# Loading the context group's query weights ahead of its output projection, and running eight expert rows before the sample norm

## The chip, the cores and the metric

The kernel runs on one core of one Trainium2 chip. The metric is device time in microseconds (us) of one execution; lower is better. 0.2% of the time before is 8.8 us.

## What is computed

The program is one step of a two-layer network over two groups of tokens: 128 context tokens (one block of 128) and 512 sample tokens (four blocks). Both groups share all weights. In each layer a mixer (layer 0: convolution and attention; layer 1: Fourier and short convolution) is followed by a channel mixer that looks up experts by product keys:

```python
def peer(h, wq, keys, u_tab, v_tab):          # per block of 128 tokens
    q = (xb @ wq).reshape(n, PEER_HEADS, 2, PEER_HALF)
    s = jnp.einsum('nhpd,hpkd->nhpk', q, keys_f)
    sv, si = lax.top_k(s, PEER_TOPK)           # 16 of 128 keys, twice
    ...
    fv, fi = lax.top_k(cand, PEER_TOPK)        # 16 of the 256 pairs
    ue = jnp.take(u_tab, eidx, axis=0)         # 16 rows of 1024 per token and head
    act = jax.nn.gelu(jnp.einsum('nhkd,nd->nhk', ue, xb))
    ve = jnp.take(v_tab, eidx, axis=0)
    return jnp.einsum('nhk,nhkd->nd', gate * act, ve)
```

There are 2 layers, 5 blocks, 8 heads and 16 experts: 1280 "rows", each of which gathers 128 rows of `peer_u` and 128 rows of `peer_v` (1 MB together) for the 128 tokens of a block.

## The kernel before, in words

**Segments, steps and rows.** A segment is the expert lookup of one block in one layer (0 to 9; segment 0 is the context block of layer 0). It has 8 steps (one per head) of 16 rows. Five engine programs are written by hand in the same order of work; each calls its own `rows(n)` at the same places, so that `n` rows are woven between two pieces of the mixer's work. The numbers stand in `RATES`, by layer and group. The mixer of the sample group in layer 0 runs inside segment 0 and the start of segment 1.

**What a row is, per engine.** GpSimd gathers a u tile into `u_ring` (8 buffers) and a v tile into `v_ring` (8 buffers); its order is fixed in `step`: four u gathers, then four v gathers that lag by 8 rows. A u gather waits until VectorE has done the dot product that used its buffer (`dots_done`); the first v gather of a step waits for ScalarE's `spread_indices` (`idx_v_done`). VectorE does the dot (`dot`, line 1714), at row 15 of a step the top-k of the step two further on (`topk`), at row 6 `weigh`, and at rows 10, 13, 0 and 4 a `diagonal` (the weights that TensorE needs). ScalarE does at row 4 `late` (gelu, exp and a load of scores), at row 8 `spread_weights`, at row 12 `spread_indices`. TensorE, at every fourth row, adds four weighted v tiles to `ps_v` (line 931, 16 matmuls), 24 rows behind. `topk` ends with a write of `idx`, which waits until ScalarE has spread the indices of the step two before.

**Weights.** SyncE (SP) issues the weight loads in program order, each a slice of 256 columns (1 MB), into slots. `w_slots` has three slots; before the gathers begin, `v_ring` gives slots 3 to 6 and `seg_bufs` slots 7 and 8 (`slot_view`). Which slice goes where, and whose last reader it waits for, is set by `plan_weights`. In `prep` each slice of `peer_wq` comes with its 128 KB of `peer_keys`.

**Around the change.** In the context group of layer 0 the order is: mixer, `mix_out` (output projection, line 1168), `norm` for `h2T`, `scores` slices 0 and 1, top-k of steps 0 and 1, then segment 0 starts: `scores` slices 2 to 7 on TensorE and ScalarE beside `rows(16)` on VectorE. Then comes the sample group: `norm` for `hT` (4 blocks), `even_a` (four chunks `vg`, which need weight slices `win` 0 and 2, then 1 and 3; line 1015), `even_qkv` (four blocks; slices 4, 5, 6; line 1047), `attend` block 0 with the convolution's taps, `conv_norm`, `mix_out`, `norm` for `h2T`, `scores` (8 slices), and `attend` block 1. In that block, after head 4, `next_segment` runs what is left of segment 0.

## Time and profile before

| | us |
|---|---|
| median of 3 runs | 4412.31 (4406.25 to 4415.29) |
| the profiled execution, its own time | 4403.28 |
| its span, first to last instruction | 4401.5 |

The page of the profile gives over the whole span: VectorE busy 61%, GpSimd 55%, TensorE 50%, ScalarE 24%; 1579 MB moved at a mean of 359 GB/s; a mean granted TensorE clock of 0.69 of full speed. In stretches with no mixer the 16 DMA engines move 409 GB/s; in segment 0, where the sample group's mixer runs, they move 147 to 394 GB/s in stretches of 25 us.

How to read it: a timeline row gives the start, the length, the engine and line, output and inputs, and in brackets how long the engine had been idle and what ended that. A row of the SP queue is the issue of a transfer, not its landing. The number of a row of work (row 0 to 127 of segment 0) isn't in the trace; it follows from counting line 1714.

### The profile page before, as it was taken

To read this page: it belongs to the slowest core of one execution; us is meant where nothing else is said; L and a number is where in the kernel's file an instruction comes from. 1 tells how busy PE (TensorE), PEld (TensorE's weight loads), DVE (VectorE), ACT (ScalarE), POOL (GpSimd) and SP (SyncE) were. 2 spreads that over 40 slices of the span, in tenths; PEclk is the share of its full clock that TensorE was granted. 3 is DMA by queue.
4 is the path that set the end of the run, shared out by engine and by line. 5 is a ranking of instruction groups with operands and counts; after the bars stand their busy time and mean duration, and the time that the engine had idled before them with its cause. 6 is when DMAs were issued, how large, how long until landed. Compare 5 with 4: busy or idle time off the path is not lost.

```text
span 4401.5 us, 39752 instructions
## 1 busy us (share of the span) xinstructions
PE 2218.3 (50%) x11314; PEld 1066.7 (24%) x11314; DVE 2696.5 (61%) x6958; ACT 1068.6 (24%) x3554; POOL 2436.0 (55%) x2564
## 2 busy tenths in 40 slices
PE   6667566667834433334653397535853333333333
PEld 4545243334412100002430134303420000000000
DVE  3546947877455666675457545475566676767672
ACT  1132223232311222221222212221322222222221
POOL 0134545455554676775367443474467776777774
PEclk8879677678966655556775599757876565556656
DMA  9688898879999999999899988999999999999997
GB/s 292 201 292 299 289 319 303 307 274 385 362 381 386 397 408 409 409 409 361 321 401 409 351 298 302 339 409 343 376 374 409 409 408 403 402 403 400 409 402 299
DMA packets 576690, 1579.06 MB, mean 359 GB/s; under 512 B 49870, under 2 KB 237230, under 8 KB 576342
## 3 DMA queue, kind: packets, MB, share of 16 engines
q0 software_dynamic: 368640, 1342.34, 78.8%
q1 hardware_dynamic: 183744, 213.28, 14.3%
q10 hardware_dynamic: 24086, 20.92, 1.4%
q8 instruction: 88, 1.44, 0.1%
q14 instruction: 132, 1.08, 0.1%
HBM read 1550.16 MB, written 26.18 MB: 358 GB/s over the span
## 4 chain that ended last, share of the span: by engine, by line
DMA 30%; PE 18%; POOL 14%; issue 10%; DVE 8%; ACT 2%; SPq 1%; POOLq 0%; ACTq 0%; DVEq 0%
DMA v_ring<-in_peer_v_dram,idx_v 13%; POOL v_ring L870 8%; PE ps_box L1015 7%; DMA u_ring<-in_peer_u_dram,idx 6%; PE ps_v L931 6%; POOL u_ring L860 6%; DMA w_slots<-in_w_mod_dram 3%; DVE u_ring L1714 2%; DMA w_slots<-in_peer_keys_dram 2%; PE ps_box L1168 1%; DMA w_slots<-in_w_out_odd_dram 1%; DMA w_slots<-in_w_in_odd_dram 1%; PE ps_box L1150 1%; DMA xa<-XM 1%; PE ps_box L972 1%
## 5 line engine op out<-in xcount | busy, mean ns | idle before, releaser
L1714 DVE CUSTOM_DVE_ANT_0 u_ring<-u_ring,h_cur 128x1024 f32<-128x1024 f32 x1280 | 1532.9, 1216 | 628.9 <-DMA u_ring<-in_peer_u_dram,idx 612.0
L860 POOL DMA_INDIRECT u_ring<-in_peer_u_dram,idx x1280 | 1216.2, 950 | 1137.7 <-DVE act_v L1714 605.4
L931 PE MATMUL ps_v<-v_ring,w_diag 128*32 128x512 f32 x5120 | 1011.5, 930 | 1485.3 <-DMA v_ring<-in_peer_v_dram,idx_v 1346.7
L870 POOL DMA_INDIRECT v_ring<-in_peer_v_dram,idx_v x1280 | 1219.5, 953 | 809.0 <-PE ps_v L931 434.6
L931 PEld LDWEIGHTS ps_v<-v_ring,w_diag 128*32 128x32 f32 x5120 | 195.5, 146 | 2210.6 <-issue 1587.0
L1015 PE MATMUL ps_box<-HT,w_slots 128*128 128x128 f32 (+2 forms) x1728 | 473.9, 437 | 61.3 <-DMA w_slots<-in_w_in_odd_dram 32.5
L1312 ACT ACTIVATE w_v<-w_tok 32x4 f32<-32x4 f32 x1280 | 265.5, 207 | 806.0 <-DVE w_tok L1772 774.5
L1015 PEld LDWEIGHTS ps_box<-HT,w_slots 128*128 128x128 f32 x1728 | 293.2, 214 | 248.6 <-issue 152.1
L1322 ACT ACTIVATE idx_v<-idx 32x4 uint32<-32x4 uint32 x1280 | 265.5, 207 | 235.2 <-PE ps_v L931 220.2
L1328 ACT ACT_TABLE_LOAD x79 | 101.4, 1283 | 372.4 <-DVE act_v L1714 354.4
L1723 DVE TENSOR_TENSOR w_diag<-w_v,eye 128x128 f32<-128x128 f32 x320 | 92.0, 288 | 142.2 <-ACT w_v L1312 125.7
L1168 PE MATMUL ps_box<-w_slots,CAT 128*128 128x256 f32 x576 | 141.3, 407 | 51.6 <-DMA w_slots<-in_w_out_odd_dram 38.8
L1168 PEld LDWEIGHTS ps_box<-w_slots,CAT 128*128 128x128 f32 x576 | 116.4, 205 | 85.3 <-issue 45.4
L1959 DVE SCALAR_TENSOR_TENSOR HT<-AR,HT 128x128 f32<-128x128 f32 (+1 forms) x360 | 129.8, 432 | 0.0
L1334 ACT ACT_TABLE_LOAD x79 | 101.4, 1283 | 92.3 <-DVE neg_max L1746 91.1
L972 PE MATMUL ps_box<-w_slots,AR 128*2 128x128 f32 x768 | 65.4, 343 | 102.2 <-DMA w_slots<-in_w_mod_dram 94.3
L1714 DVE DVE_READ_ACCUMULATOR2_ANT act_v<- 128x1 f32 x1280 | 104.7, 82 | 0.0
L2045 DVE TENSOR_TENSOR AR<-ps_box,BC 128x256 f32<-128x256 f32 x40 | 16.9, 421 | 139.5 <-PE ps_box L1168 139.5
L1772 DVE SCALAR_TENSOR_TENSOR w_tok<-gelu_v,ex_rec,ex 128x16 f32<-128x16 f32 x80 | 18.8, 235 | 119.7 <-issue 114.4
L1095 PE MATMUL ps_box<-AR,HT 128*128 128x64 f32 x336 | 61.3, 344 | 57.0 <-ACT HT L1502 55.6
L1015 PE MATMUL ps_box<-CAT,w_slots 128*128 128x128 f32 x512 | 77.3, 317 | 15.3 <-ACT XM L1567 14.2
L1508 ACT ACTIVATE HT<-ps_box 128x640 f32<-128x640 f32 (+1 forms) x40 | 24.8, 619 | 243.9 <-PE ps_box L1088 243.9
(191 smaller groups left out, 2279.0 us busy)
## 6 DMA issues: line engine op xcount, KB each, us to landing
w_slots<-in_peer_wq_dram SPq DMA_DIRECT2D x48, 1024.0 KB, 13.2
w_slots<-in_w_mod_dram SPq DMA_DIRECT2D x34, 1024.0 KB, 15.5
u_ring<-in_peer_u_dram,idx POOLq DMA_INDIRECT x1280, 12.2
v_ring<-in_peer_v_dram,idx_v POOLq DMA_INDIRECT x1280, 12.1
w_slots<-in_w_in_odd_dram SPq DMA_DIRECT2D x16, 1024.0 KB, 16.9
w_slots<-in_w_out_odd_dram SPq DMA_DIRECT2D x12, 1024.0 KB, 24.8
v_ring<-in_w_mod_dram SPq DMA_DIRECT2D x11, 1024.0 KB, 12.1
s_buf<-sc ACTq DMA_DIRECT2D x78, 128.0 KB, 5.9
```

Source lines behind the costliest of these rows:

```text
L860: pool.indirect_dma_start(out=u_ring[:, k % NU, :], out_offset=None, in_=u_rows, in_offset=bass.IndirectOffsetOnAxis(ap=idx[:, h % 2, k:k ...
L870: pool.indirect_dma_start(out=v_ring[:, k % NV, :], out_offset=None, in_=v_rows, in_offset=bass.IndirectOffsetOnAxis(ap=idx_v[:, h % 2, k: ...
L931: last = nc.tensor.matmul(ps_v[QUARTER * q:QUARTER * q + QUARTER, 512 * half:512 * half + 512], w_diag[:, c % GROUPS, q, :], v_ring[:, (r ...
L972: last = nc.tensor.matmul(out[32 * j:32 * j + 2, :], ct[:, c, :], w[:, c, j * P:(j + 1) * P], start=(c == 0), stop=(c == DC - 1))
L1015: last = nc.tensor.matmul(out, w[:, c, col:col + P], h[:, c, :], start=(c == 0), stop=(c == DC - 1))
L1168: last = nc.tensor.matmul(box[:, 0:WC], cat(b)[:, c, :], w[:, c, :], start=(c == 0), stop=(c == 7))
L1312: last = nc.scalar.activation(dst, src, ACT.Copy)
L1322: last = nc.scalar.activation(dst, src, ACT.Copy)
L1328: nc.scalar.activation(gelu_v[:, h % 2, :], act_v[:, h % 2, :], ACT.Gelu_apprx_tanh).then_inc(gelu_done, 1)
L1334: nc.scalar.activation(ex[:, h % 4, :], fv[:, h % 2, :], ACT.Exp, bias=neg_max[:, h % 2:h % 2 + 1], accum_out=ex_sum[:, h % 4:h % 4 + 1]). ...
L1714: nc.vector.tensor_tensor_reduce(u_ring[:, k % NU, :], u_ring[:, k % NU, :], h_cur[:, :], 1.0, 0.0, ALU.mult, ALU.add, act_v[:, h % 2, k:k ...
L1959: ins = nc.vector.scalar_tensor_tensor(out[:, c, :], src, cw[:, c, j:j + 1], out[:, c, :], ALU.mult, ALU.add)
```

## The change

It has five parts.

1. In `plan_weights` the eight `peer_wq` slices of the context group in layer 0 get slots 0 to 6 and 0 again (`WQ_SLOTS`), so that slices 3 to 6 lie in `v_ring`, and the order of slots after them starts anew. Their keys come as one transfer of 1 MB into `seg_bufs[:, 2:4]`.
2. On SP, the keys and slices 0 to 3 are issued before the loads of the next norm's rows (`bc_ffn`), slices 4 to 6 before `out_end` (the store of `xa`, which waits for the output projection), slice 7 behind the store of `hs`. `load_seg(0)`, whose buffers now hold the keys, moves behind the last slice that reads them.
3. GpSimd waits, between step 0 and step 1, until TensorE has used slice 6, the last one in `v_ring`.
4. ScalarE runs its 16 rows of step 0 (of which only `spread_indices` does anything) between `scores` slices 3 and 4, not behind slice 7.
5. `EARLY_ROWS`: all engines run 8 more rows before the sample group's norm; `RATES` gives them back: 4 rows for each chunk of `even_a` where it was 5, 2 in `conv_norm` where it was 4, and the last 2 rows in `next_segment` are gone.

```diff
+WQ_SLOTS = (0, 1, 2, 3, 4, 5, 6, 0)
-RATES = {(0, SMP): {"norm": 1, "vg": 5, "vg_end": 2, "qkv": 5, "attend": (3, 3, 3, 3), "conv_norm": (4, 4), "out": (1, 2),
+RATES = {(0, SMP): {"norm": 1, "vg": 4, "vg_end": 2, "qkv": 5, "attend": (3, 3, 3, 3), "conv_norm": (2, 4), "out": (1, 2),
+EARLY_ROWS = 8
...
-    early = len(FIRST_ORDER) + 4
+    first = len(FIRST_ORDER) + 4
...
-        slot = n % NWA if n < early else (n - early) % NW
+        if n < first:
+            slot = n % NWA
+        elif n < first + 8:
+            slot = WQ_SLOTS[n - first]
+        else:
+            slot = (n - first - 8) % NW
...
+            def wq_first(first, end):
+                for s in range(first, end):
+                    load_weight(sp, ("wq", 0, CTX, 0, s), T["peer_wq"][0], s * WC)
...
             sp.wait_ge(S("mod_row", 0), 8)
+            sp.dma_start(seg_bufs[:, 2:4, :].rearrange("p n d -> p (n d)").rearrange("p (j d) -> p j d", d=P),
+                         T["peer_keys"][0].rearrange("h j k d -> k (h j) d")).then_inc(S("keys_in"), 16)
             rows_out(0, 1, 3, 6)
             rows_out(0, 0, 0, 2)
+            wq_first(0, 4)
...
             load_bc(0, CTX, 3, 1, "bc_ffn")
+            wq_first(4, 7)
             out_end(0, CTX, 0)
-            prep(0, CTX, 0)
+            sp.wait_ge(S("h2_tok", 0, CTX), 1)
+            sp.dma_start(hs[0], h2_tile(0, CTX, 0)).then_inc(S("hs_out", 0, CTX), 16)
+            wq_first(7, 8)
+            sp.wait_ge(S("hs_out", 0, CTX), 16)
+            sp.wait_ge(S("xa_out", 0, CTX), 16)
+            load_h(0)
 
             mix_in(0, SMP)
             prep_end(0, CTX, 0)
+            box, use = boxes[("kyT", 0, CTX, 0, 7)]
+            sp.wait_ge(box_ready[box], use + 1)
+            load_seg(0, 0, CTX)
             even_in(SMP)
...
+            box, use = boxes[("q", 0, CTX, 0, 13)]
+            pool.wait_ge(box_ready[box], use + 1)
...
             start(0)
             third(0, 0, CTX)
+            rows(TOPK)
             scores(0, CTX, 0, 4, 8)
-            rows(TOPK)
+            rows(EARLY_ROWS)
             all_stored(0, CTX, 0)
             norm(0, SMP, "hT")
```

TensorE and VectorE have `rows(TOPK + EARLY_ROWS)` where they had `rows(TOPK)` at the start of segment 0.

How instructions stand on two engines shows it. On the SP queue, around the end of the context group's mixer (`modrow` is the table of modulation rows, `BC` its broadcasts, `in_peer_wq` and `in_peer_keys` the query weights and keys), before:

```order
L639 DMA modrow<-u_ring 2x12x128 [waits mod_row_0,mod_taken_0]
L639 DMA modrow<-u_ring 2x12x128
L639 DMA modrow<-u_ring 2x8x128 x2
L651 DMA BC<-modrow 128x1024 [waits mod_out_0,kv_out]
L651 DMA BC<-modrow 128x1024
L714 DMA xa<-XM 128x1024 [waits x_mixed_0_0]
L459 DMA w_slots<-in_peer_wq_dram 128x8x256 [waits wmod_read_0]
L461 DMA w_slots<-in_peer_keys_dram 128x2x128
```

and with the change:

```order
L800 DMA seg_bufs<-in_peer_keys_dram 128x16x128 [waits mod_row_0,mod_taken_0]
L649 DMA modrow<-u_ring 2x12x128 x2
L649 DMA modrow<-u_ring 2x8x128 x2
L469 DMA w_slots<-in_peer_wq_dram 128x8x256 [waits wmod_read_0] x3
L469 DMA v_ring<-in_peer_wq_dram 128x8x256 [waits wmod_read_0]
L661 DMA BC<-modrow 128x1024 [waits mod_out_0,kv_out]
L661 DMA BC<-modrow 128x1024
L469 DMA v_ring<-in_peer_wq_dram 128x8x256 [waits box_ready1]
L469 DMA v_ring<-in_peer_wq_dram 128x8x256 [waits box_ready0]
L469 DMA v_ring<-in_peer_wq_dram 128x8x256 [waits box_ready1]
L728 DMA xa<-XM 128x1024 [waits x_mixed_0_0]
L812 DMA hs<-CAT 128x1024 [waits h2_tok_0_0]
```

The keys and four slices stand ahead of the two `BC` loads, three more ahead of the store of `xa`, and only the eighth behind the store of `hs`.

On ScalarE, from the store of scores of slice 3 on (`AR` holds queries, keys and staged scores, `sc` is their place in memory), before:

```order
L1587 DMA sc<-AR 128x256 [waits box_free1]
L1567 ACTIVATE AR<-ps_box 128x256 [waits box_ready0,stage_out_0_0_0_1]
L1571 ACTIVATE AR<-ps_box 128x128 [waits box_ready1]
L1571 ACTIVATE AR<-ps_box 128x128 [waits box_ready0]
L1580 ACTIVATE AR<-ps_box 128x128 [waits stage_out_0_0_0_0,box_ready1]
```

and with the change:

```order
L1615 DMA sc<-AR 128x256 [waits box_free1]
L1350 ACTIVATE idx_v<-idx 32x4 [waits topk_done,stage_out_0_0_0_1]
L1350 ACTIVATE idx_v<-idx 32x4 x15
L1595 ACTIVATE AR<-ps_box 128x256 [waits box_ready0]
L1599 ACTIVATE AR<-ps_box 128x128 [waits box_ready1]
```

The spread of step 0's indices stands ahead of slice 4, no longer behind slice 7.

On ScalarE again, from the store of slice 7 to the first block of the sample norm (`CAT<-XM` is its square, `HT<-ps_box` the copy of a transposed block, `w_v` the spread weights), before:

```order
L1587 DMA sc<-AR 128x256 [waits box_free1]
L1322 ACTIVATE idx_v<-idx 32x4 [waits topk_done]
L1322 ACTIVATE idx_v<-idx 32x4 x15
L1435 ACTIVATE CAT,st<-XM 128x1024 [waits xm_in_0_1,stage_out_0_0_0_1,stage_out_0_0_0_0]
L1436 ACT_TABLE_LOAD
L1436 ACTIVATE st<-st,eps 128x1 [waits act_chain]
L1435 ACTIVATE CAT,st<-XM 128x1024
L1436 ACTIVATE st<-st,eps 128x1 [waits act_chain]
L1458 ACTIVATE HT<-ps_box 128x8x128 [waits box_ready0]
```

and with the change:

```order
L1615 DMA sc<-AR 128x256 [waits box_free1]
L1356 ACT_TABLE_LOAD
L1356 ACTIVATE gelu_v<-act_v 128x16 [waits dots_done]
L1362 ACT_TABLE_LOAD
L1362 ACTIVATE ex,ex_sum<-fv,neg_max 128x16 [waits negmax_done]
L1380 DMA s_buf<-sc 128x256 [waits topk_done]
L1463 ACTIVATE CAT,st<-XM 128x1024 [waits xm_in_0_1,stage_out_0_0_0_1,stage_out_0_0_0_0]
L1464 ACT_TABLE_LOAD
L1464 ACTIVATE st<-st,eps 128x1 [waits act_chain]
L1463 ACTIVATE CAT,st<-XM 128x1024
L1464 ACTIVATE st<-st,eps 128x1 [waits act_chain]
L1486 ACTIVATE HT<-ps_box 128x8x128 [waits box_ready0]
```

Gelu, exp and a load of scores now stand between the last slice and the norm, and `spread_weights` inside the norm; both stood in `even_a`.

## Rows read from the trace of the kernel before

**Rows 1.** The page's DMA queues: packets, MB, share of 16 engines.
```profile
q0 software_dynamic: 368640, 1342.34, 78.8%
q1 hardware_dynamic: 183744, 213.28, 14.3%
```

**Rows 2.** Windows: busy us per engine, granted PE clock, DMA share, GB/s.
```profile
150.00:175.00 25.00, 18.92 (x75) 15.69 (x74) 5.53 (x11) 5.21 (x8) 0.00 (x0) 0.75 0.00 1
...
250.00:275.00 25.00, 11.41 (x71) 9.86 (x70) 9.77 (x14) 13.16 (x37) 3.80 (x2) 0.70 0.76 260
...
350.00:375.00 25.00, 16.47 (x76) 9.53 (x74) 14.22 (x31) 7.49 (x23) 16.58 (x18) 0.93 0.95 351
```

**Rows 3.** Timeline of ScalarE: start us, us, operation, [idle before <-releaser].
```profile
234.14 0.38 ACT L1567 ACTIVATE AR<-ps_box 128x256 f32<-128x256 f32 x1 [6.39 <-DMA sc<-AR]
...
258.82 3.49 ACT L1322 ACTIVATE idx_v<-idx 32x4 uint32<-32x4 uint32 x16 [0.42 <-ACT AR L1580]
```

**Rows 4.** Timeline of VectorE, 262 to 269 us, same columns.
```profile
262.42 0.17 DVE L1764 TENSOR_SCALAR idx<-abf 128x16 uint32<-128x16 f32 x1 [19.94 <-ACT idx_v L1322]
...
265.19 0.16 DVE L1876 RECIPROCAL st<-st 128x1 f32<-128x1 f32 x1 [2.60 <-ACT st L1436]
...
267.85 1.21 DVE L1714 CUSTOM_DVE_ANT_0 u_ring<-u_ring,h_cur 128x1024 f32<-128x1024 f32 x1
```

**Rows 5.** Timeline of GpSimd, its gathers, 233 to 287 us.
```profile
233.46 0.94 POOL L860 DMA_INDIRECT u_ring<-in_peer_u_dram,idx  x1 [0.59 <-DVE act_v L1714]
...
269.34 1.94 POOL L860 DMA_INDIRECT u_ring<-in_peer_u_dram,idx  x1 [34.95 <-DVE act_v L1714]
...
285.69 0.94 POOL L870 DMA_INDIRECT v_ring<-in_peer_v_dram,idx_v  x1 [0.30 <-issue]
```

**Rows 6.** Timeline of the SP queue, loads of the sample projection's slices.
```profile
260.20 2.75 SPq L459 DMA_DIRECT2D w_slots<-in_w_in_even_dram  x3
...
314.29 40.73 SPq L459 DMA_DIRECT2D w_slots<-in_w_in_even_dram  x3
```

**Rows 7.** Timeline of TensorE, 282 to 376 us.
```profile
282.45 29.13 PE L1015 MATMUL ps_box<-HT,w_slots 128*128 128x512 f32 x64 [1.11 <-ACT HT L1458]
...
315.48 3.16 PE L931 MATMUL ps_v<-v_ring,w_diag 128*32 128x512 f32 x16 [3.89 <-DVE w_diag L1723]
322.24 15.97 PE L1015 MATMUL ps_box<-HT,w_slots 128*128 128x512 f32 x32 [3.59 <-issue]
338.14 1.92 PE L931 MATMUL ps_v<-v_ring,w_diag 128*32 128x512 f32 x16
...
375.78 14.08 PE L1047 MATMUL ps_box<-w_slots,HT 128*128 128x256 f32 x64 [2.66 <-DMA w_slots<-in_w_in_even_dram]
```

**Rows 8.** Timeline of VectorE in the sample attention, 432 to 473 us.
```profile
432.56 0.22 DVE L1919 RECIPROCAL st<-st 128x10 f32<-128x10 f32 x1 [2.90 <-ACT st L1486]
...
462.70 0.29 DVE L1728 MAX8 sv<-s_buf 128x8 f32<-128x128 f32 x1
...
472.16 0.17 DVE L1764 TENSOR_SCALAR idx<-abf 128x16 uint32<-128x16 f32 x1
```

**Rows 9.** Timeline of TensorE where the sample output projection starts.
```profile
566.86 9.71 PE L1168 MATMUL ps_box<-w_slots,CAT 128*128 128x256 f32 x32 [6.79 <-ACT CAT L1528]
```

**Rows 10.** Timeline of ScalarE, SP queue, TensorE, 586 to 626 us.
```profile
586.48 1.06 ACT L1435 ACTIVATE CAT<-XM 128x1024 f32<-128x1024 f32 x1 [16.29 <-DVE XM L2048]
...
595.56 0.71 SPq L725 DMA_DIRECT2D hs<-CAT  x1
...
606.71 0.38 ACT L1567 ACTIVATE XM<-ps_box 128x256 f32<-128x256 f32 x1 [11.54 <-DMA hs<-CAT]
...
625.98 0.69 PE L1182 MATMUL ps_box<-ident,w_slots 128*128 128x128 f32 x2 [10.75 <-DMA w_slots<-in_peer_keys_dram]
```

**Rows 11.** Timeline of VectorE and TensorE, 679 to 697 us.
```profile
679.00 0.82 DVE L1970 TENSOR_REDUCE st<-ps_box 128x1 f32<-128x640 f32 x1 [18.47 <-PE ps_box L1077]
...
696.14 1.30 PE L1088 MATMUL ps_box<-ident,HT 128*128 128x128 f32 x5 [8.16 <-DVE HT L1990]
```

More of the change, by code:

```diff
@@ L188, in mix @@
             for s in range(8):
-                order.append((("wq", l, g, q, s), ("q", l, g, q, 2 * s + 1), 2))
+                order.append((("wq", l, g, q, s), ("q", l, g, q, 2 * s + 1), 1 if (l, g) == (0, CTX) else 2))
     mix(0, CTX)
@@ L448, in weight_keys @@
         def weight_keys(key):
+            if key[1:3] == (0, CTX):
+                at = 2 * P * key[4]
+                return seg_bufs[:, 2:4, :].rearrange("p n d -> p (n d)")[:, at:at + 2 * P].rearrange("p (j d) -> p j d", j=2)
             return w_slots[:, weights[key][0], DC * WC:DC * WC + 2 * P].rearrange("p (j d) -> p j d", j=2)
@@ L727, in prep @@
                         sp.wait_ge(S("xa_out", l, g), 16 * hi)
-                        if (l, g) == (0, CTX):
-                            load_h(0)
-                            load_seg(0, 0, CTX)
-                        elif g == SMP:
+                        if g == SMP:
                             load_h(5 * l + 1 + q)
@@ L884, in step @@
                             gather_v(i - 1, h - 1, k - V_LAG)
-            for i in range(16):
-                step(i // 8, i % 8, first=i == 0)
+            step(0, 0, first=True)
+            box, use = boxes[("q", 0, CTX, 0, 13)]
+            pool.wait_ge(box_ready[box], use + 1)
+            for i in range(1, 16):
+                step(i // 8, i % 8)
             with Segments(pool, 2, 4, per_seg) as seg:
@@ L1178, in scores @@
                     w = weight(pe, ("wq", l, g, q, s))
+                    if (l, g) == (0, CTX):
+                        pe.wait_ge(S("keys_in"), 16)
                     kr = weight_keys(("wq", l, g, q, s))
@@ L1217, in _ @@
             scores(0, CTX, 0, 2, 8)
-            rows(TOPK)
+            rows(TOPK + EARLY_ROWS)
             turn_h(0, SMP, "hT", "h_tok")
@@ L1621, in _ @@
             third(0, 0, CTX)
+            rows(TOPK)
             scores(0, CTX, 0, 4, 8)
-            rows(TOPK)
+            rows(EARLY_ROWS)
             all_stored(0, CTX, 0)
@@ L2070, in _ @@
             start(0)
-            rows(TOPK)
+            rows(TOPK + EARLY_ROWS)
             norm(0, SMP, "hT")
```

## The prediction

> **What bounds the kernel now.** I read the page first, then windows of 25 us over the first 800 us, then each engine's timeline from 120 to 745 us, since all that the change touches lies there. From the start of segment 1 on, both programs are the same, every wait there is on another engine or on a transfer, and nothing waits for a fixed time: what segment 0 gains or loses should reach the end whole. So the sum is made of the points where segment 0 waits.
>
> Two idle stretches stand out. Between 150 and 175 us the transfers are idle (share 0.00) while the context group's mixer ends [rows 2]. Later VectorE waits 19.94 us with the top-k of step 2 finished but for its write of `idx`, because ScalarE spreads step 0's indices only behind slice 7, at 258.82 [rows 3, 4]. GpSimd in that time stands still for 34.95 us, since no dot frees a buffer [rows 5]. The reader is to see that it isn't the transfers that limit here: in 250 to 275 us they run at 260 GB/s [rows 2]. Behind it, in the sample mixer, limits alternate: TensorE in `even_a` (29.13 us of matmuls for two chunks, 15.97 for the third) [rows 7], then the landing of slices, then VectorE through `even_qkv` and `attend`, where a top-k takes 472.16 - 462.70 = 9.5 us [rows 8].
>
> **The change part by part.** All shifts are changed kernel minus before.
>
> *Early weights.* Some 9 MB of slices and keys move into the idle stretch. That alone gives little: slices 0 and 1 weren't waited for, and the first dots hang on two top-ks that hang on the projection. Slices 4 to 7 take ScalarE (258.8 - 234.1) / 4 = 6.2 us each with waits for keys in them [rows 3]; without these I take 5. ScalarE reaches slice 4 at 234.14, after 6.39 us for a store of scores [rows 3]; with fewer weights in the queues this store may come 0 to 3.5 us sooner. Add the 3.49 us spread and four slices: the last slice ends at about 254.5 to 258.5, against 258.8 before.
>
> *The new wait on GpSimd.* The gathers of step 1 (16 to 31) are held until slice 6 is used, about 6 us before the last slice ends: 248.6 to 252. Before, gathers up to 23 were out at 234.4 [rows 5]; this is what comes late in place of the spread. Behind it on GpSimd stands every later gather, v too. At 0.94 + 0.30 = 1.24 us a gather [rows 5] gather 23 is issued at 257.6 to 261 and lands an estimated 5 us later (a store through busy queues took 6.39), so dot 23 ends at 263.7 to 267. Of the 20 us that VectorE waited, the wait keeps most, but eight dots now lie in it.
>
> *The norm.* Before, VectorE starts it at 265.19 [rows 4]. ScalarE must now do gelu and exp first (about 4 us, two table loads), which ends at 258.5 to 263, and the norm's square and root take 2.9 (262.3 to 265.19) [rows 3, 4]: no later than the dots. Its four blocks are unchanged. In it TensorE now has the first v sum, 3.2 us at half clock [rows 7], and ScalarE a 3.5 us spread. `even_a` needs slices `win` 0 and 2, issued at about 260 as before [rows 6], but now beside some 20 gathers. I take a start 2.5 us later than 282.45 [rows 7]; bounds -1 (the store is quick) and +10.
>
> *even_a.* TensorE's chunks stay. Two v sums (rows 31 and 35 where one stood) lie about the first pair; the first adds 1.9 [rows 7], the second lies under the load of slice 3, which is issued when chunk 1 is done: that sets the start of chunk 2 at 322.24, 10.6 us behind 311.6 [rows 7]. The wait of 3.89 us on the diagonal goes, and is worth nothing, since the load ends last. The end of chunk 3 is then +1.9. Next come slices 5 and 6, issued by 314.29 + 40.73 = 355.0 [rows 6] and awaited until 375.78 [rows 7]: 21 us, with 18 gathers issued in 350 to 375 us at a transfer share of 0.95 [rows 2, 7], because a top-k (row 31) had dammed up the dots of chunk 2. It now falls into chunk 0, where VectorE is idle; I count 12 gathers in that stretch and take 3 us less. Together -1; bounds -6 and +2.
>
> *even_qkv.* With four rows more done, both rows 47 and 63, each with a top-k, fall in it, where one did. VectorE is the chain here: +9.5. The 2.90 us wait on ScalarE's root [rows 8] goes, as gelu and spreads move to blocks with cover: +6.6; bounds +3 and +9.5.
>
> *attend, block 0.* One top-k where two stood: -9.5, and with VectorE less full 1 us of other waits shows: -8.5; bounds -9.5 and 0.
>
> *conv_norm.* Two dots less (2.3 us), and row 88, a spread of 3.5 us on ScalarE just ahead of the last activation, moves forward into `attend`; a v sum moves behind the variance. The output projection waited 6.79 us for ScalarE here [rows 9]. -4.5; bounds -6 and 0.
>
> *mix_out and the second norm.* The v sum inside the four chunks moves behind them: -2. But row 95 with its top-k now stands between the mixed x (586.48) and the norm, 7.6 us more for the norm. ScalarE's slices don't start from the norm, however, but from the landing of the store of `hs`: it is issued at 595.56, 9.1 us after the mixed x, behind two slices, and lands 11 us later, at 606.71 [rows 10]. Issued 13.3 us after, with those slices mostly landed, it should take 5 to 10 us: -1 for this. -3 in all; bounds -6 and +7.6.
>
> *scores.* Eight slices with two rows each as before, limited by landings (10.75 us for one [rows 10]): 0; bounds -4 and +4.
>
> *attend, block 1, head 0.* The top-k of row 111 stood here, and TensorE waited 8.16 us for VectorE; now it falls into the slices, where VectorE is idle for 18.47 us at their end [rows 11]. -8; bounds -9.5 and 0.
>
> *next_segment.* Two dots fewer before segment 1, 1.14 us each at VectorE's pace: -2.3.
>
> Sum: 2.5 - 1 + 6.6 - 8.5 - 4.5 - 3 + 0 - 8 - 2.3 = -18.2 us. The profiled execution took 4403.28, 9 us under the median; its span would be 4383, its own time 4385, and the median 4412.3 - 18.2 = **4394 us**. As 0.2% (8.8 us) is about what a measurement of this kernel tells from no change, this is faster. A check from the other side: eight dots (9.2 us) and one top-k leave the stretches where VectorE is the chain, 18.7 us.
>
> **A rule against it.** In the load of slices 5 and 6 before, about 2 MB took 21 us beside gathers that never paused, near 100 GB/s [rows 6, 7]. The page's queues have mean packets of 3.6 KB for gathers and 1.2 KB for SP's loads [rows 1]. The Trainium skill ("DMA: Bandwidth & Descriptors", Queues, rings and completion order) says that each DMA engine goes round its queues by packet; one to one this would leave SP a quarter of 400 GB/s, and by that rule the trace agrees. With the gathers' burst on `win` 0 and 2 this rule alone would put the sum near -13.
>
> **The rivals.**
>
> *A. The burst holds up the first slices of the sample projection* (a chance of 0.2). Gathers 16 to 31 with v 0 to 7 now run without a pause from 250 to 280, where the trace has GpSimd idle. The segment's own loads (1 MB) and `win` 0 and 2 share with them. At the 21 us for 2 MB above, and 5 us for the segment's loads, `win` 2 lands at 286 to 290, so `even_a` starts 4 to 8 us late, and slice 3 may lose 2 more. Against it: the burst ends at about 280. Sum: -18.2 + 5 = about 4399, bounds 4395 to 4406.
>
> *B. The top-ks land on the path and none leaves it* (0.12, slower). The shift by four and two rows moves top-ks as follows: one into `even_qkv` (+6.6), one between mixed x and norm (+7.6 if the store of `hs` follows the norm by its 11 us as before). If block 0 of `attend` and head 0 of block 1 turn out to be held by TensorE and ScalarE and give nothing: 2.5 - 1 + 6.6 + 0 - 4.5 - 2 + 7.6 + 0 + 0 - 2.3 = +6.9, and with `conv_norm` giving nothing +11.4: 4419 to 4424. It decides when the two attentions give back less than 5 of their 16.5 us. Against it: VectorE has hardly a gap in them.
>
> *C. Little change* (0.18). Some of the gains are real but a landing ends last behind them: the slices of `scores` are limited by transfers, and if the same bytes need the same time whenever they start, the shift is halved or lost there: 4404 to 4416.
>
> *D. More* (0.1). Quick stores, the early slices also freeing the queues, bounds taken on the good side: -26 to -35, 4377 to 4386.
>
> The forecast itself has 0.4, with a range of 4386 to 4400.
>
> **How the numbers follow.** Faster by over 0.2% (under 4403.5): the forecast, D and nearly all of A give 0.4 + 0.1 + 0.18 = 0.68. Within 0.2%: C and the rest of A, 0.2. Slower: B, 0.12. The range leaves out the slower half of C and B at the top, and little below: 4379 to 4413.
>
> **What would show it.** In the changed kernel's profile: the loads of `peer_wq` between 141 and 171 us and a share above 0.7 in place of 0.00; ScalarE's first spread at 231 to 238; VectorE's write of the third `idx` without a wait at 239 to 243, then a wait of 9 to 14 us for the gather of row 16, ended by a transfer; GpSimd idle until about 250 and then 24 gathers in a row; `even_a` at 284 to 287; two top-ks in `even_qkv` and one in the first `attend`; no wait of TensorE on VectorE in the first head of block 1. The prediction is wrong if the wait for `win` 2 or for `hs` is longer than it was by more than 8 us, or if segment 0 ends at the same time as before with these steps as described, which would mean that a landing I took as hidden sets its end.

## The result, and the profile after

The changed kernel takes 4422.47 us (median of 8 runs, 4411.85 to 4426.40), the kernel before 4411.15 us (8 runs beside it, 4403.61 to 4415.41): ratio 1.0027, 95% interval 1.0017 to 1.0037, or some 11 us **slower**. I had forecast 18 us faster. The profiled execution took 4420.41 us with a span of 4418.6 us, at the same mean granted clock (0.69).

The early part went as forecast. Windows of the kernel after (columns as in [rows 2]):

```profile
150.00:175.00 25.00, 19.71 (x79) 16.50 (x77) 4.88 (x9) 5.49 (x9) 0.00 (x0) 0.73 0.89 291
250.00:275.00 25.00, 7.18 (x43) 6.03 (x42) 17.50 (x28) 13.55 (x35) 19.01 (x20) 0.61 1.01 390
275.00:295.00 20.00, 7.09 (x33) 4.11 (x34) 7.88 (x13) 5.99 (x10) 11.22 (x11) 0.59 1.04 395
350.00:375.00 25.00, 21.29 (x57) 8.25 (x55) 6.05 (x13) 5.96 (x10) 7.51 (x8) 0.93 0.57 200
```

The idle stretch of the transfers is filled (share 0.89 where it was 0.00), but from 250 to 295 us they are full: 390 GB/s, where [rows 2] had 260. Timelines of the kernel after, of ScalarE, VectorE, GpSimd and the SP queue, which answer to [rows 3 to 6]:

```profile
230.02 3.49 ACT L1350 ACTIVATE idx_v<-idx 32x4 uint32<-32x4 uint32 x16 [2.57 <-DMA sc<-AR]
...
252.34 1.22 DVE L1743 CUSTOM_DVE_ANT_0 u_ring<-u_ring,h_cur 128x1024 f32<-128x1024 f32 x1 [11.91 <-DMA u_ring<-in_peer_u_dram,idx]
...
275.49 0.16 DVE L1905 RECIPROCAL st<-st 128x1 f32<-128x1 f32 x1 [3.06 <-ACT st L1464]
...
247.72 0.94 POOL L883 DMA_INDIRECT u_ring<-in_peer_u_dram,idx  x1 [24.63 <-PE ps_box L1041]
...
260.44 17.74 SPq L469 DMA_DIRECT2D w_slots<-in_w_in_even_dram  x3
```

The spread is at 230.02, VectorE's wait is now for the gather of row 16, and GpSimd starts at 247.72 and then issues 28 gathers without a pause, until 284.6. That was in the forecast but for the length of the run of gathers: I had named 24, with an end at about 280. Then it goes another way. Timeline of TensorE after, which answers to [rows 7]:

```profile
294.66 16.53 PE L1041 MATMUL ps_box<-HT,w_slots 128*128 128x512 f32 x32 [7.60 <-DMA w_slots<-in_w_in_even_dram]
315.08 3.64 PE L957 MATMUL ps_v<-v_ring,w_diag 128*32 128x512 f32 x16 [3.89 <-DVE w_diag L1752]
318.65 14.80 PE L1041 MATMUL ps_box<-HT,w_slots 128*128 128x512 f32 x32
336.20 2.56 PE L957 MATMUL ps_v<-v_ring,w_diag 128*32 128x512 f32 x16 [2.75 <-DVE w_diag L1752]
338.89 14.90 PE L1041 MATMUL ps_box<-HT,w_slots 128*128 128x512 f32 x32
356.54 2.42 PE L957 MATMUL ps_v<-v_ring,w_diag 128*32 128x512 f32 x16 [2.75 <-DVE w_diag L1752]
358.89 15.15 PE L1041 MATMUL ps_box<-HT,w_slots 128*128 128x512 f32 x32
379.08 3.21 PE L957 MATMUL ps_v<-v_ring,w_diag 128*32 128x512 f32 x16 [5.04 <-DVE w_diag L1752]
...
601.64 6.35 PE L1194 MATMUL ps_box<-w_slots,CAT 128*128 128x256 f32 x16 [6.70 <-DMA w_slots<-in_w_out_even_dram]
```

`even_a` starts 12.2 us later than in [rows 7], behind a slice (`win` 2) that was issued right after 260.44 and lands some 34 us later. In it stand four v sums, and each waits for a diagonal (3.89, 2.75, 2.75 and 5.04: 14.4 us, against 6.1 before). And the last chunk of the output projection waits 6.70 us for slice `wout` 3, where there was no wait. VectorE's timeline in `even_qkv` shows where each block of tokens begins:

```profile
394.79 0.82 DVE L1944 TENSOR_TENSOR CAT<-CAT 128x640 f32<-128x640 f32 x1 [11.87 <-ACT AR L1511]
...
420.32 0.83 DVE L1944 TENSOR_TENSOR CAT<-CAT 128x640 f32<-128x640 f32 x1 [3.30 <-ACT AR L1511]
...
439.89 0.83 DVE L1944 TENSOR_TENSOR CAT<-CAT 128x640 f32<-128x640 f32 x1 [6.49 <-ACT AR L1511]
...
456.96 0.83 DVE L1944 TENSOR_TENSOR CAT<-CAT 128x640 f32<-128x640 f32 x1 [2.64 <-ACT AR L1511]
...
484.58 0.82 DVE L1999 TENSOR_REDUCE st<-ps_box 128x1 f32<-128x640 f32 x1 [5.09 <-PE ps_box L1103]
```

Blocks 0 and 3 hold a top-k (25.5 and 27.6 us) and block 2 none (17.1), but block 1, which has none either, takes 19.6 us and ends in 6.49 us of idle time.

With such starts (of the norm, `even_a`, the first block of `even_qkv`, the first head of `attend`, `mix_out`, ...) segment 0 can be cut into stretches. Each number is what a stretch adds to the shift against the kernel before, in us, and the last row is the sum, up to the copy of `h_cur` for segment 1 (730.08 before, 748.49 after). The other columns are kernels of the next section.

| stretch | after | e1 | e4 | e9 | e13 | e14 | e15 |
|---|---|---|---|---|---|---|---|
| up to the norm's start | -0.4 | -5.8 | +2.5 | -3.6 | -3.2 | -1.5 | -2.2 |
| norm, wait for `win` | +12.7 | 0 | +5.4 | +12.9 | +11.9 | +13.7 | +3.2 |
| `even_a`, first keys | +2.1 | +1.2 | -1.6 | -5.6 | -6.4 | +15.5 | -2.6 |
| `even_qkv` | +11.7 | 0 | +10.9 | +9.1 | +17.5 | +9.0 | +10.6 |
| `attend`, block 0 | -4.9 | +0.5 | -6.1 | -8.3 | -3.7 | -9.2 | -8.4 |
| `conv_norm` | -3.6 | -0.3 | -3.6 | -4.5 | -3.6 | -1.2 | -3.6 |
| `mix_out` | +5.0 | -0.2 | +4.8 | -0.4 | -0.2 | -4.1 | 0 |
| second norm, `scores` | -1.9 | -0.3 | -3.9 | -5.9 | +4.2 | +1.9 | -4.6 |
| `attend`, block 1, four heads | -2.1 | +2.2 | -3.3 | -1.2 | -3.7 | -1.2 | -2.4 |
| end of segment 0 | +18.4 | -2.8 | +5.1 | -7.4 | +12.7 | +22.8 | -10.1 |

A profile is one execution: e4 and a twin of it (e10) with the same program up to `conv_norm` start the norm 3.6 us apart, so a single entry is good to some 4 us. The last row has about the order of the medians and not their size: it is up to 10 us above the difference of the medians (after, e13 and e15 by 7 to 10), as the profiled execution of the kernel before was 8 us faster than its median, and that of e13 the slowest of its 12.

### The profile page after: what moved, and what is told of

It reads as the page before. It is cut to its first block, busy times and chain, and to the rows that moved or that the text cites. A ratio compares the mean times of both kernels' runs of the same rounds, so it can differ in the third digit from the quotient of the medians.

```text
span 4418.6 us, 39748 instructions
## 1 busy us (share of the span) xinstructions
PE 2234.1 (51%) x11314; PEld 1071.4 (24%) x11314; DVE 2698.2 (61%) x6958; ACT 1068.6 (24%) x3554; POOL 2444.9 (55%) x2564
## 4 chain that ended last, share of the span: by engine, by line
DMA 30%; PE 18%; POOL 11%; DVE 10%; issue 9%; ACT 2%; SPq 1%; POOLq 0%; DVEq 0%; ACTq 0%
DMA v_ring<-in_peer_v_dram,idx_v 13%; DMA u_ring<-in_peer_u_dram,idx 7%; POOL v_ring L893 7%; PE ps_box L1041 7%; PE ps_v L957 6%; POOL u_ring L883 5%; DMA w_slots<-in_w_mod_dram 3%; DVE u_ring L1743 3%; DMA w_slots<-in_peer_keys_dram 2%; PE ps_box L1194 1%; DMA w_slots<-in_w_out_odd_dram 1%; DMA w_slots<-in_w_in_odd_dram 1%; SPq L471 1%; PE ps_box L1176 1%; PE ps_box L998 1%
## 5 line engine op out<-in xcount | busy, mean ns | idle before, releaser
L1041 PE MATMUL ps_box<-HT,w_slots 128*128 128x128 f32 (+2 forms) x1600 | 453.6, 446 | 48.5 <-DMA w_slots<-in_w_in_odd_dram 26.2
L1041 PEld LDWEIGHTS ps_box<-HT,w_slots 128*128 128x128 f32 x1600 | 273.1, 211 | 236.7 <-issue 156.5
L2074 DVE TENSOR_TENSOR AR<-ps_box,BC 128x256 f32<-128x256 f32 x40 | 16.9, 423 | 145.5 <-PE ps_box L1194 145.5
L1041 PEld LDWEIGHTS ps_box<-CAT,w_slots 128*128 128x128 f32 x512 | 78.2, 243 | 21.0 <-ACT XM L1595 11.7
## 6 DMA issues: line engine op xcount, KB each, us to landing
u_ring<-in_peer_u_dram,idx POOLq DMA_INDIRECT x1280, 12.1
v_ring<-in_peer_v_dram,idx_v POOLq DMA_INDIRECT x1280, 12.1
v_ring<-in_w_mod_dram SPq DMA_DIRECT2D x11, 1024.0 KB, 12.1
```

The source lines that it names most:

```text
L1041: last = nc.tensor.matmul(out, w[:, c, col:col + P], h[:, c, :], start=(c == 0), stop=(c == DC - 1))
```

## Experiments

Fifteen kernels, each timed beside the kernel before.

**Loads or rows.** Two theories at first: that gathers in a burst keep `win` 2 from landing, or that the rows stand badly. e1 takes the rows out of the changed kernel, e2 adds to the kernel before the earlier spread alone, e3 adds spread, eight rows and rates without the loads, e4 issues `win` 2 and 1 early.

```diff
 # e1, from the changed kernel
-                   "vg": 4, ... "conv_norm": (2, 4)
+                   "vg": 5, ... "conv_norm": (4, 4)
-EARLY_ROWS = 8
+EARLY_ROWS = 0
 # e2, from the kernel before (e3: also rows(EARLY_ROWS), and the new rates)
+            rows(TOPK)
             scores(0, CTX, 0, 4, 8)
-            rows(TOPK)
 # e4, from the changed kernel; even_in leaves out 2 and 1
             mix_in(0, SMP)
+            for s in (2, 1):
+                load_weight(sp, ("win", 0, SMP, s), T["w_in_even"][0], s * WC)
```

> The changed kernel without its eight early rows: EARLY_ROWS is 0 and the rates of vg and conv_norm are those of before, so that only the earlier weights and keys, GpSimd's wait and the earlier spread are left. Two theories of the 11.3 us that the change lost. Burst theory: the run of gathers from 250 us on keeps the slices win 0 and 2, issued at 260 us, from landing, and even_a's late start (12.2 us) is nearly the whole loss. Then even_a starts here not before 284 us although VectorE has eight dots less to do ahead of the norm and ends the norm by 276, and the kernel takes 4410 to 4418. Rows theory: the loss comes from where the v sums and top-ks of the eight rows fall (w_diag waits in even_a, two top-ks in even_qkv, a late wout 3). Then even_a starts at 276 to 282, later stretches are as in the kernel before, and the kernel takes 4402 to 4408.

> The kernel before, with ScalarE's spread of step 0's indices moved ahead of slices 4 to 7 and nothing else. Gathers 16 and on then go out as dots free their buffers, from about 242 us, in place of 269. Both theories: the norm can start when ScalarE has done slice 7, at 258 to 262 in place of 265.2. Burst theory: win 0 and 2, issued at 260, are met by fewer gathers (16, mostly issued by 262), so that even_a starts at 276 to 281 and the kernel takes 4404 to 4409, faster by 2 to 7 us. Rows theory says nothing else here. If the landing of win 2 sets even_a's start at 282 or later all the same, neither the burst nor the norm's start is what counts, but the time of issue at 260.

> The kernel before, with the earlier spread, the eight early rows and the new rates, but with weights and keys where they were and with no wait on GpSimd. Gathers 16 to 23 are out by 234, so that the early dots can run at 243 to 253, in VectorE's idle time. Burst theory: even_a starts at 280 to 285 and the rest is as I first worked it out, so that the kernel takes 4393 to 4403, the best so far. Rows theory: even_a starts at that time too, but the v sums wait for the diagonals of their own chunk (14 us in four waits in the changed kernel), even_qkv holds two top-ks and wout 3 comes late, so that the start of the x_mixed of mix_out is 6 to 12 us later against even_a's start than in the kernel before, and the kernel takes 4408 to 4420.

> The changed kernel, with the loads of win 2 and win 1 of the sample group issued behind the loads of the sample blocks, as soon as slices wq 1 and 2 are used (by about 220 us, 40 us ahead of before and ahead of the gathers). Their slots are free then. Only win 0 still waits for wq 7. Burst theory: with one slice in place of three beside the burst, even_a starts by 284 to 288, held by the norm's end (283.3) or by win 0, and 7 to 10 us come through to the end: 4412 to 4416. Rows theory: even_a starts as early, but the chunks then wait longer for diagonals and VectorE, and less than 4 us reach the end: 4418 to 4423.

Measured: e1 4408.23 us (ratio 0.9999, 0.9989 to 1.0009); e2 4406.70 (0.9994, 0.9985 to 1.0002); e3 4414.15 (1.0010, 1.0001 to 1.0020); e4 4415.43 (1.0012, 1.0004 to 1.0021). The loads, GpSimd's wait and the spread alone cost nothing and bring nothing that can be measured (e1, e2; VectorE starts e2's norm at 264.87, where 258 to 262 was expected, as the spread waits 6.22 us for a store of scores). Eight rows with the old loads are already slower than before (e3, where I had once forecast a gain), and early `win` slices give the changed kernel some 6 us back (e4, by the ratios). So both theories hold in part: by e4 the late slices are about half of the loss, and the rows are the other half.

In e1 the norm starts 5.8 us earlier than before, and TensorE then waits for no slice (`even_a` at 276.62). The late `win` of the changed kernel is thus not due to GpSimd's wait alone: without early dots only 8 gathers go out in a row, with them 28.

**Which of the rows.** e5 takes the rows out of the norm and puts five in each chunk of `even_a`; e6 has seven early rows in place of eight; e7 lightens `even_qkv`; e8 has no early rows and six in each chunk. All four have e4's early `win` slices.

```diff
 # e5                                    # e7 adds "qkv": 4, "conv_norm": (4, 4)
-{"norm": 1, "vg": 4,
+{"norm": 0, "vg": 5,
 # e6
-EARLY_ROWS = 8
+EARLY_ROWS = 7
 # e8, from e1
-{"norm": 1, "vg": 5,
+{"norm": 0, "vg": 6,
```

> e4_win_early (the changed kernel with win 2 and 1 loaded early) with no row in the sample norm and five in each chunk of even_a (norm 0, vg 5), so that after even_a the rows stand as in e4. Norm theory (from the traces of e1, e3 and e4): with eight early rows the norm starts about 8 us later than without, and in it the row that is a multiple of 16 plus 8 puts a spread of w_v (3.5 us) into ScalarE's way, so that the norm takes 21.1 us in place of 15.7. Without rows it takes 11 to 13 us: even_a starts at 280 to 283 in place of 290.4, the v sums no longer stand behind the last dot of their own chunk, and waits on w_diag fall from 14.4 to under 6 us: even_a ends 10 to 16 us earlier than in e4 and the kernel takes 4400 to 4408. Diagonal theory (the v sums' waits are what counts, the norm is hidden behind the landing of win 0): even_a starts at 286 to 290 and 5 to 8 us are won inside even_a: 4407 to 4412. If neither helps, VectorE's load alone sets the time and it takes 4413 to 4417.

> e4_win_early with seven early rows in place of eight (EARLY_ROWS 7): every v sum of even_a then stands behind the first row of a chunk, whose diagonal was made in the chunk before, and the weighing of row 24 (which waits for ScalarE's gelu behind slice 7) moves out of the stretch ahead of the norm. Diagonal theory: the four waits of v sums on w_diag (3.89, 2.75, 2.75, 5.04 us) go, even_a is 8 to 14 us shorter, and the kernel takes 4403 to 4408. Norm theory: only the start of the norm moves, by one dot and the wait on gelu, even_a's chunks stay 19 to 21 us apart, because VectorE's work on each chunk and not the v sum sets their distance: 4411 to 4415.

> e5_bare_norm with qkv 4 in place of 5 and conv_norm (4, 4) in place of (2, 4), so that even_qkv has rows 46 to 61 with one top-k, and from attend of block 0 on the rows stand as in the kernel before. If the chance placing of top-ks behind even_a costs nothing in sum (they only move), this gives what e5 gives less four dots in even_qkv, plus what block 0 of attend had gained: within 3 us of e5. If the late top-k between mixed x and norm (7.6 us) and the late wout 3 (6.3 us wait) are what the changed kernel loses behind even_a, this is 4 to 8 us faster than e5: 4394 to 4402.

> The other way round: early weights, early spread and early win 2 and 1, but no early rows at all (EARLY_ROWS 0, rates norm 0, vg 6, conv_norm (4, 4)), so that rows 16 to 39 lie in even_a and all behind it is as in the kernel before. Norm theory: the norm starts at 261 as in e1 and takes 11 to 13 us, so that even_a starts at 272 to 275, against 282.5 before and 276.6 in e1; six dots a chunk (6.9 us) still fit beside 14 us of matmuls, and the kernel takes 4398 to 4405, the fastest yet. Against it: if the landing of win 0, issued at 257, sets the start, even_a starts at 276 or later and nothing is gained over e1 (4408); if six dots and VectorE's own work on a chunk are more than 15 us, the chunks grow by 1 to 3 us each and it takes 4406 to 4412.

Measured: e5 4408.74 us (1.0002, 0.9989 to 1.0015); e6 **4397.43** (0.9973, 0.9961 to 0.9985); e7 4412.29 (1.0010, 0.9996 to 1.0023); e8 4424.39 (1.0035, 1.0019 to 1.0051). e5 takes the time of the diagonal theory, but not for its reason: `even_a` starts at 283.3, as the norm theory had it, 7.1 us ahead of e4, and the median follows (7 us under e4's). The further gain that the norm theory had inside `even_a` didn't come, as three v sums still wait for diagonals there (12.1 us together). e7, with the rows behind `even_qkv` as in the kernel before, is no faster than e5, so that by this run their new place costs nothing in sum: e7's profile is 15 us shorter than e5's in `even_qkv` and 5 in `mix_out`, and 13 us longer in `attend` of block 0 with `conv_norm`, 4 in the second norm and `scores`, and 5 in block 1. e8 is 12 us above even the slower of its two cases (4412): its v sums wait 7.66, 3.89 and 3.18 us, as six dots stand ahead of or beside each diagonal. The surprise is e6: one row fewer is worth 17 us, more than all four waits on diagonals.

**One row alone.** e9 is the changed kernel with seven early rows and nothing else, e11 the same on the old loads (e3). e10 takes two rows out of `conv_norm` of e4. e12 puts the v sums right with three early rows.

```diff
 # e9 and e11
-EARLY_ROWS = 8
+EARLY_ROWS = 7
 # e10, from e4
-"conv_norm": (2, 4)
+"conv_norm": (0, 4)
 # e12, from e1
-EARLY_ROWS = 0            "vg": 5, "vg_end": 2
+EARLY_ROWS = 3            "vg": 4, "vg_end": 3
```

> The changed kernel with EARLY_ROWS 7 in place of 8 and nothing else. In e6 this one row gave 17 us over e4 (4397.4 against 4415.4). Theory now: a v sum on TensorE that stands in the same step as the dot that makes its diagonal on VectorE stalls TensorE; with eight rows all four of even_a's do, with seven none but the last; and one row fewer brings row 91's v sum into mix_out's first chunk and row 95's top-k behind the second norm. Then this kernel has even_a's chunks without waits on w_diag, no wait for wout 3, and takes 4398 to 4408; the late landing of win 2 stays, so that it is 3 to 8 us behind e6 (4397). If early win 2 and 1 were what made seven rows work, it takes 4412 or more.

> e4_win_early (eight early rows) with conv_norm (0, 4) in place of (2, 4): two rows fewer ahead of mix_out, so that from there on the rows stand as in the kernel before (v sum of row 91 inside mix_out, row 95's top-k behind the second norm, row 111's in the first head of attend, two rows left for next_segment). If the late wout 3 (6.25 us wait) and that top-k (7.6 us ahead of the norm) are part of the loss, mixed x comes 5 to 8 us earlier than in e4 and the kernel takes 4406 to 4412; the top-k of row 111 takes back up to 8 us of it in block 1. If what is behind even_qkv costs nothing in sum, it takes 4413 to 4418 as e4.

> e3_rows_only (the kernel before with the earlier spread and the new rates, old loads, no wait on GpSimd) with seven early rows in place of eight. Theory now: the four waits on w_diag and the late wout 3 go as in e6, and the kernel takes 4397 to 4404, so that the early loads of weights and keys are worth nothing for the gain (e6: 4397). If the early loads count (norm and even_a earlier), it takes 4405 to 4410.

> e1_no_early_rows with three early rows (EARLY_ROWS 3) and rates vg 4, vg_end 3: the v sums of rows 27, 31, 35 and 39 stand behind the first row of a chunk, as in e6, and all behind even_a is as in the kernel before. Only three dots lie ahead of the norm, in time in which VectorE waits anyway (gathers 16 to 18 land by 254, ScalarE's square root for the norm comes at 259.4 in e1). So the norm starts at 260 to 262 and even_a at 276 to 278 as in e1, even_a is 3 to 6 us shorter than in e1, and the kernel takes 4398 to 4405. If it takes 4406 or more, the v sums' place is worth little by itself and the gain of e6 came from behind even_qkv.

Measured: e9 4401.29 us (0.9981, 0.9970 to 0.9992); e10 4418.52 (1.0022, 1.0013 to 1.0030); e11 4402.24 (0.9976, 0.9966 to 0.9986); e12 4416.62 (1.0014, 1.0004 to 1.0023). So the row is what counts, and the early loads are not needed for it (e11 is as fast as e9). TensorE's waits of 286 to 400 us, kernel after (engine, line, waited for: us in total, times, longest):

```profile
PE ps_v L957 <- DVE w_diag L1752: 14.4, 4, 5.0
PE ps_box L1041 <- DMA w_slots<-in_w_in_even_dram: 7.6, 1, 7.6
```

and the same stretch of e9:

```profile
PE ps_box L1041 <- DMA w_slots<-in_w_in_even_dram: 10.9, 1, 10.9
PE ps_box L1041 <- issue: 5.3, 1, 5.3
PE ps_v L957 <- DVE w_diag L1752: 4.3, 1, 4.3
```

The late slice is there in both; the waits on diagonals are gone but for one. e10 shows the other half: with row 91 in `mix_out` the wait for `wout` 3 is gone there too (`mix_out` 5.3 us shorter than e4's), but more than that is lost again. Row 111's top-k falls into block 1 again (3.4 us in the profiles), and the second norm and `scores` take 6.9 us more, with a wait of 8.76 us for the keys of the third slice that e4 doesn't have. My expectation had only the first of these. e12 is a miss, and it speaks against the v sums as the whole story: of their waits in `even_a` one of 2.04 us is left, and the kernel is still some 7 us slower than e1 by the ratios. Its profile has gelu and exp inside the norm, where TensorE waits 5.98 us, so that `even_a` starts at 285.38, and slices 5 and 6 are waited for 6.95 us, in e1 1.02 us. 3.9 us of the later start were there at ScalarE's first spread already (231.44 against 227.54), with the same program up to it, so they are the difference of two executions.

**V sums or dots.** In e13 TensorE alone is one row behind (23 rows at the start, 24 on VectorE and ScalarE), in e14 one ahead (24 against 23). e15 is e9 with `win` 2 and 1 issued once `wq` 4 is used.

```diff
 # e13, TensorE's program only
-            rows(TOPK + EARLY_ROWS)
+            rows(TOPK + EARLY_ROWS - 1)
 # e14, EARLY_ROWS = 7, TensorE's program only
+            rows(TOPK + EARLY_ROWS + 1)
 # e15, from e9; even_in leaves out 2 and 1
             mix_in(0, SMP)
+            box, use = boxes[("q", 0, CTX, 0, 9)]
+            sp.wait_ge(box_ready[box], use + 1)
+            for s in (2, 1):
+                load_weight(sp, ("win", 0, SMP, s), T["w_in_even"][0], s * WC)
```

> The changed kernel with TensorE alone one row behind: it goes through 23 rows at the start where VectorE and ScalarE go through 24, so that dots, weighings and top-ks stand where they do in the changed kernel and only the v sums stand one row later against them (each of even_a's stands a chunk after its diagonal). Alignment theory: of the 21 us between eight and seven early rows (4422 and 4401), the part that is due to v sums is even_a's (8.5 us by the traces), up to 3 us in even_qkv, and wout 3 with the v sum ahead of mix_out (5.4 us): 4405 to 4412. Top-k theory: what seven rows gain lies in where the top-ks and dots stand (rows 63, 95 and 111), and this takes 4415 to 4422.

> The reverse: seven early rows on VectorE and ScalarE, as in e9_seven_rows_alone, but eight on TensorE, so that each v sum of even_a again stands in the chunk in which its diagonal is made, while dots and top-ks stand as in e9. Alignment theory: the waits on w_diag come back, with one more dot to wait for, and wout 3 is late again: 12 to 18 us of e9's gain are lost, 4413 to 4422. Top-k theory: 4401 to 4406 as e9.

> e9_seven_rows_alone with win 2 and win 1 issued when slice wq 4 is used, at about 237 us: in e9 the transfers move 57 GB/s between 235 and 250 us, while the gathers are held back, and TensorE waits 10.87 us for win 2, until 291.80. In e4 the same two loads at 195 us slowed the stores of scores on which ScalarE waits (5.9 in place of 2.7 us) and put the norm's start 3 to 6 us back. Issued here 2 MB land by 246. Burst theory: even_a starts at 282 to 286 in place of 291.8 and the kernel takes 4392 to 4398. If a later landing or VectorE then sets the pace, and the 8 us are taken back in even_qkv and attend, it takes 4399 to 4402.

Measured: e13 4413.83 us (1.0007, 0.9996 to 1.0017); e14 4428.63 (1.0039, 1.0025 to 1.0053); e15 **4390.62** (0.9960, 0.9946 to 0.9975), 20 us faster than before in its own comparison and the fastest of all. e13 lies between its two theories, e14 6 us above the upper bound of the alignment theory, and e15 just under its range. TensorE's waits in e14, same stretch:

```profile
PE ps_v L957 <- DVE w_diag L1752: 28.5, 4, 13.4
PE ps_box L1041 <- DMA w_slots<-in_w_in_even_dram: 8.1, 1, 8.1
```

With dots and top-ks where e9 has them, putting the v sums one row forward costs 25 us. With the dots of the changed kernel, putting them one row back gives 9 us (ratio 1.0027 to 1.0007). Of the 20 us between eight rows and seven, a little under half is the v sums' own; the rest is where the dots and top-ks stand, and how the two meet: e13's profile has 6 us more than the changed kernel's in `even_qkv`, where a spread on ScalarE now waits for a late v sum. ScalarE and VectorE of e13:

```profile
438.45 3.49 ACT L1350 ACTIVATE idx_v<-idx 32x4 uint32<-32x4 uint32 x16 [9.32 <-PE ps_v L957]
...
442.30 0.22 DVE L1948 RECIPROCAL st<-st 128x10 f32<-128x10 f32 x1 [5.79 <-ACT st L1514]
```

In e15 `even_a` starts at 283.38 without a wait for a slice, 8.4 us earlier than in e9, and the median is 9 us better by the ratios (0.9981 to 0.9960, on 6 runs and with intervals that just overlap; the trace is the stronger evidence).

## Why the prediction was wrong

The terms of the forecast add up to -18.2 us and the stretches of the profile to +18.4, so the prediction is off by 36.6 us. Five steps make nearly all of it: the start of `even_a` (9.7), `attend` of block 1 (8.1), the output projection (7.0), `even_qkv` (5.1) and `attend` of block 0 (3.6). The step that failed most is the first: the overlap of slice `win` 2 with the gathers, for which the sum had a start 2.5 us later and the runs show 12.2. Behind part of the rest stands a wait that the sum put at nothing, that of the v sums for their diagonals.

**Right:** that the idle stretch fills, that the last slice ends a few microseconds sooner (253.8, just under my 254.5), VectorE's 12 us for the gather of row 16, GpSimd's wait, the norm's unchanged start, two top-ks in `even_qkv`, 4.5 us in `conv_norm` (3.6), the 7.6 us that row 95's top-k puts ahead of the second norm and the quicker store of `hs` that takes them back (-1.0 in sum, as forecast), no change in `scores`, the 2.3 us of `next_segment` (head 4 up to the copy of `h_cur` takes 4.7 us where it took 7.0), and that what segment 0 has at its end comes through (18.4 us there, 17.1 in the span).

**"A start 2.5 us later"** measured 12.2, over the upper bound of 10. The sum followed the norm and gave the burst a chance of 0.2 and 4 to 8 us as rival A. The rate was right: 2 MB of slices and 1 MB of the segment's own in 34 us are 88 GB/s, near the 100 that I had read off slices 5 and 6. My burst was too short: I had it end at about 280, and 3 MB at 100 GB/s from 260.4 would have been 291. The count of 24 gathers left out four u gathers for which the norm's dots free the buffers. Rival A's mechanism is shown by e15 (`win` 2 issued in a pause, no wait) and is worth 8 to 9 us, in e15 against e9. DMA queues of the kernel after, 270 to 294.66 us (packets, MB, share of 16 engines; q0 has the gathers, q1 SP's loads):

```profile
q0 software_dynamic: 2088, 7.61, 79.2%
q1 hardware_dynamic: 2088, 2.11, 24.5%
```

Packet for packet the two queues got the same number, and with 3.6 KB against 1.0 KB a packet SP's share of the bytes is 22%. The Trainium skill ("DMA: Bandwidth & Descriptors", Queues, rings and completion order) has the queues take turns by packet, and this trace agrees. My own sign of being wrong, a wait for `win` 2 over 8 us longer than before, wasn't even reached: the wait is 7.60 us, as TensorE came out of the norm 4.6 us later than before. Also left out of the sum was the norm itself: a spread for row 24 stands on ScalarE between its roots, and VectorE waits 3.06 us there, but the landing hides it.

**"The wait of 3.89 us on the diagonal goes"**, and is worth nothing, is the mechanism that failed. It did not go, there were four such waits (14.4 us in place of 6.1). A diagonal of row 29 is made by VectorE in the very chunk behind which TensorE's v sum of row 31 stands, so that TensorE must sit out VectorE's first dots of the chunk. With eight rows and four a chunk, every v sum of `even_a` stands behind the last row of its chunk; with seven, behind the first, and its diagonal is a chunk old. I counted how many v sums stand there and what each costs in matmuls (1.9 us), and not which row of the step makes what they need. `even_a` to the first keys measured +2.1 (I had -1), against -5.6 in e9. e13 and e14 show it: moving the v sums alone moves this stretch by 8.5 and 21 us.

**"even_qkv +6.6"** measured 11.7. The second top-k costs its 9.5 (e9: +9.1), and the 2.9 us that I took off for a root wait did not come: another wait, 3.9 us longer than it was, took its place (6.49 at the end of block 1, where 2.64 stood). A wait that moves isn't a wait that goes.

**"attend, block 0, -8.5"** measured -4.9 and in e9 -8.3, so the price was right for rows that stand well. **"mix_out -2"** measured +5.0: slice 3 is issued at 588.07, into gathers with no pause above 2.5 us, and lands 13.6 us later, where before it was issued at 573.15 in a pause of GpSimd of 7.7 us and nobody waited. In e9 and e13, with the v sum of row 91 inside `mix_out`, the wait is gone. That a pause of the gathers is what makes the slice quick fits all 17 kernels: the four with a wait (after, e3, e4, e5) have no pause above 4.0 us near the issue, the others one of 6.6 us or more (e14 too, with its v sum ahead: 597.32, in a pause of 9.4 us). It was not tried by itself.

**"attend, block 1, head 0, -8"** gave 4.5 us in head 0 (16.9 us to 12.4), and heads 1 to 3 took them back (27.2 to 31.8). Timeline of ScalarE after, in heads 2 and 3:

```profile
724.23 3.48 ACT L1340 ACTIVATE w_v<-w_tok 32x4 f32<-32x4 f32 x16
...
734.45 3.48 ACT L1350 ACTIVATE idx_v<-idx 32x4 uint32<-32x4 uint32 x16
```

Each spread stands a head earlier than before (713.76 in head 3, 724.98 in head 4). Head 2, which had none, takes 10.2 us in place of 7.2, head 1 10.4 in place of 9.0, and head 3 11.2 in place of 11.0; in all three VectorE now waits for TensorE, by up to 2.08 us at once where it was at most 1.02. So ScalarE's spread fits as the cause of most of it, but that was not tried; I had taken one wait of 8.16 us for the whole story.

Rival B (top-ks land on the path, none leaves it) had the right range, 4419 to 4424, by luck and not by its cause: top-ks did leave both attentions. The two causes that were found, the burst and the v sums, are A and one that I hadn't listed. What stays open is the part of the row's 20 us that e13 does not give back, 11 us by the ratios. Between e9 and e13 the table has it in `even_qkv` (8.4 us), `attend` of block 0 (4.6) and the second norm and `scores` (10.1), which with e13's slow profiled execution is more than the medians have; between e9 and the changed kernel the same three are 2.6, 3.4 and 4.0. Which dot or top-k is to blame in each was not separated.

## What to carry to other kernels

Where two engines interleave the same list of background work by count, a shift by one item can change which engine waits for which. So look, for each item that has a partner on another engine, whether the partner's half stands in an earlier step, and try the neighbours of the number chosen (8 lost 11 us, 7 won 9) before judging the idea. That alone isn't enough: with three early rows (e12) the v sums stood well too, and nothing was won. And a load that is short of time goes out in a pause of the gathers: the same two slices cost nothing at 237 us and 8 us at 260, but with them at 195 us ScalarE waited 5.8 to 5.9 us for its second store of scores in all six such kernels, and 2.1 to 3.2 us in the kernels with early `wq` slices that issue them later.

## What the runs showed of the hardware

TensorE often pays for a wait twice. Its v sum of 16 matmuls takes 1.92 us behind a chunk of matmuls, and behind the four waits of 2.75 to 5.04 us in the changed kernel 2.42 to 3.64 us, so that such a wait cost up to 1.7 us more than its length. It isn't so each time: behind a wait of 2.75 us in e4 and one of 3.18 us in e13 the v sum took 1.92 us. A chunk that follows a stretch in which TensorE mostly waits is slow as well: the first chunk takes 16.53 us in the changed kernel, behind the wait of 7.60 us, and 16.82 us in e15 directly behind the norm, with a wait of only 1.11 us, where e4's, with a v sum ahead of it, takes 14.00. The granted clock is 0.59 from 275 to 295 us, where TensorE mostly waits, near the lower of its two levels (1.2 GHz), and 0.93 from 350 to 375 us, where it is busy, near the upper (2.4 GHz). I had known the two prices of a v sum from the profile before, and had not charged the difference to the waits.

Two queues under load shared the engines by packets and not by bytes: from 270 to 294.66 us of the changed kernel the gathers' queue and SP's moved 2088 packets each, of 3.6 KB and 1.0 KB, and so SP got 22% of the bytes.
